# Reordering six steps of the first part's mixing stage on VectorE, ScalarE and TensorE

## The chip, the cores and the metric

The kernel runs on one core of one Trainium2 chip. The metric is the device time of one execution in microseconds (us), the median over several executions. One more execution is recorded by the hardware profiler; its trace gives start and length of each instruction on the five engines: TensorE (PE; PEld is its weight load), VectorE (DVE), ScalarE (ACT), GpSimd (POOL) and SyncE (SP, which here only issues DMAs).

## The reference, cut to what matters

Two blocks follow one another over a sequence of 512 tokens of width 1024. Each has two layers. The change lies in the first block, in the part of each layer called mixing, so it runs twice.

```
h = rms_norm(x, attn_norm[l])
proj = h @ w_in[l]
mq, mk, mv, mo, mi, mf, cq, ckv, krope, cu, cv = split_cols(proj, IN_SIZES)
qk = silu(causal_depthwise_conv(concat([mq, mk]), m_conv_w[l], m_conv_b[l]))   # 4 taps
hm = mlstm_chunkwise(q, k, v, mi + gb, mf + gb)          # 4 heads of 96
hm = sigmoid(mo) * hm
ha = mla_mixer(cq, ckv, krope, ...)                      # 6 heads, causal attention, latents 256 and 128
hc = chunk_spatial_gating(gelu(cu), gelu(cv), ...)       # 4 groups of 64
y = concat([head_rms_norm(hm), head_rms_norm(ha), head_rms_norm(hc)])
x = x + y @ w_out[l]
x = x + hier_moe(rms_norm(x, ffn_norm[l]), ...)          # 32 experts, top 2
```

The change alters no arithmetic except the order in which the eight chunks of `y @ w_out` are summed in the first half of the output columns.

## The kernel before

**Tiling.** The sequence is four token tiles of 128 (t = 0 to 3, `TT`), the width is eight chunks of 128 (k, `KC`). Everything is float32. Each engine runs its own program; all five are produced by the same Python functions, which are called once with each engine's name, so the order of the calls in `mixing` and `first_out` is the order of the work on every engine. Engines meet only at semaphores.

**PSUM banks.** In mixing a ring of six banks is handed out in call order (`next_bank`, `open_bank`). TensorE, when it opens bank number q, waits until bank q-6 has been read by the engines that are listed as its readers ("act", "dve" or "both"). So a reader that is late holds TensorE back six banks further on. At the output projection the ring has eight banks.

**Mixing, in call order.** Here are the parts that the change touches, by name.

- `lat_product` and `lat_read`: the latents. `conv_tile(i)`, i = 0 to 7: TensorE makes a 96x512 tile of the convolution's input from eight chunks, ScalarE reads the bank twice (L536 to a padded buffer `pads[i % 3]`, L537 to `conv` with bias and the last tap), VectorE adds the other three taps (L544, three instructions, from SBUF alone). ScalarE may write `pads` again once `conv_done` says that VectorE has finished tile i-3.
- `lat_turn(t)`: three transposes of a latent tile (L460), read by VectorE (L465). `gate_rows`: eight small transposes (L476), two VectorE reads (L479), one more VectorE instruction (L482), after which ScalarE takes Exp and Ln (L485, L487).
- `up_tile(t)`: the attention's up projections, four banks per token tile: two for q, one for k, one for v. ScalarE squares (L574, L587) or copies (L603), VectorE multiplies by the gain (L577, L590) and sums the squares (L593, L594), GpSimd takes the inverse root (L607, L608, L610) and signals `head_root`.
- `up_scale(t)`: VectorE alone, waits for `head_root` of its tile, then L620 to L622 and the rotation (L366 to L372).
- `gate_scans`: VectorE alone, L494 to L502. `gate_columns`: TensorE waits for the end of the scans, then eight tiny transposes (L515).
- `conv_silu`: ScalarE waits for all eight convolution tiles and applies Silu to all of them in place (L554).
- `head_turn(h)`: TensorE transposes q and k of an attention head (L638), ScalarE copies q out of its bank (L282), VectorE copies k (L284). `a_scores` of that head needs both copies.
- Then a loop of 12 steps: a token tile of v, u and v of the gating, or the output gate (`tok_tile`), two units of attention (`a_scores`, `a_turn`, `a_output`), and a third of an mLSTM head (`m_decay`, `m_scores`, `m_output`).
- The end of mixing: `norm_scale` of the gating's output `gu` (VectorE L888), `m_output(3)` (TensorE L780, VectorE L786 to L794), the last two `a_output` (L699; L704, L706), `heads_sums(2)` (ScalarE square L870, VectorE sum L874, GpSimd root L877 and L879), `gate_outputs` (VectorE L1058, four), `norm_sums` of the mLSTM output (the same lines L870, L874, L877, L879 again), `heads_scale(2)` (VectorE L888), then `out_turn` for chunks 6, 7, 3, 4, 5 (TensorE L898, even chunks read by VectorE L285, odd ones by ScalarE L282).
- `first_out`: the output projection. Its first half makes the products of the chunks `early` = (6, 7, 3, 4, 5) for four token tiles (TensorE L1071), then the transposes of chunks 0, 1, 2, then their products. VectorE adds each finished bank to `x`. The last transposes also release the first expert's weights (`big_free`, SP L1529).

All four calls of `key_rotation` run on GpSimd at the start of mixing. Waits of a queue hold all that stands behind them on that engine.

Of the kernel before, what the change touches and what calls it, by code (L numbers as in the profile page):

```python
# [8 lines left out]
TT = S // P  # L9
# [9 lines left out]
QK_TILES = 2 * M_HEADS  # L19
# [55 lines left out]
def program(nc, a):  # L75
# [5 lines left out]
    with ctx:  # L81
# [386 lines left out]
        def gate_rows(name, eng, l):  # L468

            gb = p1(l, "gate_b")  # L470
            H = slice(0, M_HEADS)
            for i, dst in ((0, log_i), (1, cum_f)):
                q, f = next_bank(name, "dve")
                if name == "pe":
                    o = 416 + i * M_HEADS
                    pe_job(eng, q, (T.transpose(bank_of(q)[H, t * P:(t + 1) * P], lat[:, t, o:o + M_HEADS], ident) for t in range(TT)))  # L476
                if name == "dve":
                    eng.wait_ge(bank_full, f + 1)
                    V.tensor_scalar(dst, bank_of(q)[H, :], gb[H, i:i + 1], None, ALU.add).then_inc(bank_read_dve, 1)  # L479
            if name == "dve":  # L480
                eng.drain()
                V.scalar_tensor_tensor(out=peak, in0=cum_f, scalar=-1.0, in1=cum_f, op0=ALU.mult, op1=ALU.min).then_inc(gate_neg, 1)  # L482
            if name == "act":
                eng.wait_ge(gate_neg, l + 1)
                A.activation(peak, peak, ACT.Exp)  # L485
                eng.drain()
                A.activation(peak, peak, ACT.Ln, bias=1.0).then_inc(gate_soft, 1)  # L487
# [36 lines left out]
        def conv_tile(name, eng, l, i, w):  # L524

            q, f = next_bank(name, "act")
            bank = bank_of(q)
            cw = p1(l, "conv_w").rearrange("p (t j) -> p t j", t=QK_TILES)
            n = l * QK_TILES + i
            if name == "pe":  # L530
                pe_job(eng, q, product(bank[M, :], lambda k: w[:, k, (i % 4) * M_DIM:(i % 4 + 1) * M_DIM], lambda k: featv[:, k, :], KC))
            if name == "act":
                eng.wait_ge(bank_full, f + 1)
                if i >= 3:
                    eng.wait_ge(conv_done, n - 2)
                A.activation(pads[i % 3][M, CONV - 1:], bank[M, :], ACT.Copy)  # L536
                A.activation(conv[M, i, :], bank[M, :], ACT.Identity, bias=p1(l, "conv_b")[M, i:i + 1],  # L537
                             scale=cw[M, i, CONV - 1:CONV]).then_inc(bank_read_act, 1)
            if name == "dve":
                if i == 0:  # L540
                    eng.wait_ge(pads_zeroed, l + 1)
                eng.wait_ge(bank_read_act, reads_of[q]["act"])
                for j in range(CONV - 1):
                    m = V.scalar_tensor_tensor(out=conv[M, i, :], in0=pads[i % 3][M, j:j + S], scalar=cw[M, i, j:j + 1],  # L544
                                               in1=conv[M, i, :], op0=ALU.mult, op1=ALU.add)
                    if j < CONV - 2:
                        eng.drain()
                m.then_inc(conv_done, 1)
# [63 lines left out]
        def up_scale(name, eng, l, t):  # L612

            if name != "dve":
                return
            half = A_ROPE // 2
            qh, kh = (v[:, t, :].rearrange("p (h w) -> p h w", w=A_QK) for v in (q_lat, k_lat))
            eng.wait_ge(head_root, l * TT + t + 1)
            rq, rk = head_ss[:, t, 0:6], head_ss[:, t, 6:12]
            V.tensor_tensor(qh, qh, rq.unsqueeze(2).to_broadcast([P, A_HEADS, A_QK]), ALU.mult)  # L620
            V.tensor_tensor(kh[:, :, 0:A_NOPE], kh[:, :, 0:A_NOPE], rk.unsqueeze(2).to_broadcast([P, A_HEADS, A_NOPE]), ALU.mult)
            V.tensor_tensor(kh[:, :, A_NOPE:], key_rope[:, t, :].unsqueeze(1).to_broadcast([P, A_HEADS, A_ROPE]),  # L622
                            rk.unsqueeze(2).to_broadcast([P, A_HEADS, A_ROPE]), ALU.mult)
            eng.drain()
            c, s = (r[:, t, :].unsqueeze(1).to_broadcast([P, A_HEADS, half]) for r in (cos1, sin1))
            work = [view(heads[:, 0, :], k * A_HEADS * half, A_HEADS, half) for k in range(4)]
            rotate(eng, qh[:, :, A_NOPE:A_NOPE + half], qh[:, :, A_NOPE + half:], c, s, work, half)
            eng.drain().then_inc(heads_scaled, 1)
# [275 lines left out]
        def mixing(name, eng, l):  # L904
# [51 lines left out]
            for t in range(TT):  # L956
                lat_turn(name, eng, l, t)
            gate_rows(name, eng, l)
            conv_tile(name, eng, l, 1, w)
            if l == 0 and name == "pe":  # L960
                eng.wait_ge(par_loaded[0], 16)
            up_tile(name, eng, l, 0)
            up_tile(name, eng, l, 1)
            conv_tile(name, eng, l, 2, w)
            up_scale(name, eng, l, 0)
            up_scale(name, eng, l, 1)
            up_tile(name, eng, l, 2)
            up_tile(name, eng, l, 3)
            gate_scans(name, eng, l)
# [6 lines left out]
            for i in range(M_HEADS, QK_TILES):  # L976
                conv_tile(name, eng, l, i, w)
            slot_done(name)
            conv_silu(name, eng, l)
            head_turn(name, eng, l, 0)  # L980
            for i in range(3 * TT):
                kind, t = ("m_val", "uv", "o")[i // TT], i % TT
                if t == 0:
# [27 lines left out]
            a_turn(name, eng, l, A_UNITS - 2)  # L1011
            a_turn(name, eng, l, A_UNITS - 1)
            gate_values(name, eng, l)
            m_output(name, eng, l, M_HEADS - 1)
            a_output(name, eng, l, A_UNITS - 2)
            a_output(name, eng, l, A_UNITS - 1)
            norm_scale(name, eng, l, gu, C_GROUPS, C_DIM, c_ss, c_norm)
            a_last = heads_sums(name, eng, l, 2)
            gate_outputs(name, eng, l)
            m_norm = norm_sums(name, eng, l, o_gate, M_HEADS, M_DIM, view(tmp, M_HEADS * S, TT, M_WIDTH), m_ss, outputs_gated(l))  # L1020
            heads_scale(name, eng, l, 2, a_last)
            if name == "pe":
                eng.wait_ge(a_out_read, (l + 1) * A_HEADS)
                set_ring(eng, range(8))
# [36 lines left out]
        def first_out(name, eng, l, m_norm):  # L1061
# [17 lines left out]
            if name == "pe":  # L1079
                y_squares.extend([0] * TT)  # L1080
                banks = [open_bank(eng, until=(half_added, l * TT + t + 1)) for t in range(TT)]
                for k in early:
                    reader = "act" if k % 2 else "dve"
                    eng.wait_ge(bank_read_act if k % 2 else bank_read_dve, reads_of[at["outT", k]][reader])
                    for t in range(TT):
                        products(banks[t], t, w, (k,))
            else:
                q = take(name, "bank", TT)
# [2 lines left out]
                out_turn(name, eng, l, o_gate, c, c, m_norm)  # L1091
            if name == "pe":
                big_free.append(count[("pe", "full")])
                eng.wait_ge(bank_read_act, reads_of[at["outT", 2]]["act"])
                eng.wait_ge(bank_read_dve, reads_of[at["outT", 2]]["dve"])
            for t in range(TT):
# [2473 lines left out]
```

## Time and profile before

| | |
|---|---|
| median of 3 executions | 3090.44 us (3090.29 to 3095.34) |
| profiled execution, its time | 3090.09 us |
| its span in the trace | 3088.3 us |
| PE busy | 2881.2 us, 93% of the span |
| DVE, ACT, POOL busy | 1133.3, 669.8, 518.6 us (37%, 22%, 17%) |
| mean granted clock of TensorE | 0.977 of full |
| mixing and first output half, first layer | about 14 to 301 us of the span |
| the same, second layer | about 659 to 939 us |

The page of the profile gives busy time by engine over the whole span; a kernel whose TensorE is busy 93% of the time still has stretches in which it waits, and these are found in the order of time. The 1.8 us between the profiled execution's time and its span lie outside the trace. In the rows a line such as "L406" is the line of a helper (here the generator that all products go through), so the place is read from the operands and the start. One product of float32 shows as two records.

### The profile page before, as it was taken

Reading aid. Unit: us, or ns where it says so; the run is one execution under the profiler, and the core shown is the slowest. Engines: PE = TensorE matmul, PEld = TensorE weight load, DVE = VectorE, ACT = ScalarE, POOL = GpSimd, SP = SyncE. Lnnn points to the kernel's source line nnn. Section 1 sums busy time; section 2 is a strip of 40 time slices with the busy share of each in tenths; the row PEclk is TensorE's granted clock in tenths of the full one; section 3 lists DMA queues with packets and bytes.
Section 4 is the critical chain, followed back from the end, with each engine's and each line's share of the span. In section 5 each row is a group of like instructions: output and inputs, shape, how many; then the busy total and the mean of one; then the engine's idle time right before and its main releaser. Section 6 shows DMA issues by size and latency. Waiting matters only on the chain.

```text
span 3088.3 us, 32675 instructions
## 1 busy us (share of the span) xinstructions
PE 2881.2 (93%) x12660; PEld 1928.4 (62%) x12660; DVE 1133.3 (37%) x2314; ACT 669.8 (22%) x1520; POOL 518.6 (17%) x789
## 2 busy tenths in 40 slices
PE   8999998889999988899999999999998899999998
PEld 4465543244656433377657488888685556688887
DVE  3534311135343111234623234344346732333354
ACT  3332210023232100101631211100204622211100
POOL 3001111121011111112310012210213610011201
PEclk9999999899999999899999999999999999999999
DMA  3113599941115999722012022222221021122122
GB/s 147 48 48 147 216 405 411 413 169 48 40 50 220 369 418 412 305 82 82 1 55 82 28 82 82 97 76 87 82 82 55 1 82 55 55 90 102 69 75 89
DMA packets 121908, 421.38 MB, mean 136 GB/s; under 512 B 9232, under 2 KB 13456, under 8 KB 95504
## 3 DMA queue, kind: packets, MB, share of 16 engines
q1 hardware_dynamic: 108528, 383.62, 32.5%
q0 software_dynamic: 12640, 33.45, 2.9%
q8 instruction: 106, 1.74, 0.2%
q10 hardware_dynamic: 576, 2.10, 0.2%
q14 instruction: 58, 0.48, 0.0%
HBM read 408.64 MB, written 27.26 MB: 141 GB/s over the span
## 4 chain that ended last, share of the span: by engine, by line
PE 81%; DMA 9%; DVE 4%; ACT 2%; issue 2%; DVEq 1%; POOLq 0%; POOL 0%; SPq 0%; ACTq 0%
PE ps L2359 33%; PE ps L406 14%; PE ps L2592 6%; DMA ring_feat<-in_w 6%; PE ps L1591 4%; PE ps L1071 4%; DMA big<-in_w 3%; PE ps L1631 2%; PE ps L2466 2%; PE ps L2612 2%; PE ps L2909 2%; PE ps L1843 1%; PE ps L1854 1%; PE ps L1866 1%; PE ps L2751 1%
## 5 line engine op out<-in xcount | busy, mean ns | idle before, releaser
L406 PE MATMUL ps<-ring_feat 128*96 128x512 f32 (+3 forms) x768 | 308.4, 558 | 11.0 <-DVE tmp L465 4.4
L2359 PE MATMUL ps<-ring_feat 128*128 128x256 f32 x1216 | 276.9, 379 | 0.8 <-ACT big L282 0.8
L2359 PE MATMUL ps<-big 128*128 128x256 f32 x1200 | 268.1, 379 | 0.0
L2359 PEld LDWEIGHTS ps<-ring_feat 128*128 128x128 f32 x1216 | 231.0, 190 | 33.4 <-issue 2.1
L2359 PEld LDWEIGHTS ps<-big 128*128 128x128 f32 x1200 | 228.0, 190 | 31.0
L406 PEld LDWEIGHTS ps<-ring_feat 128*128 128x128 f32 (+1 forms) x768 | 140.4, 185 | 163.7 <-issue 122.2
L2592 PE MATMUL ps<-ring_feat 128*128 128x512 f32 x448 | 194.6, 593 | 2.9 <-ACT ring_feat L2809 2.2
L1591 PE MATMUL ps<-big,tmp 128*64 128x512 f32 x512 | 126.3, 644 | 33.7 <-DMA big<-in_w 30.8
L2592 PEld LDWEIGHTS ps<-ring_feat 128*128 128x128 f32 x448 | 84.2, 190 | 106.7 <-issue 101.9
L1591 PE MATMUL ps<-ring_feat,tmp 128*64 128x512 f32 x512 | 125.0, 638 | 27.1 <-DMA ring_feat<-in_w 25.0
L1606 DVE TENSOR_TENSOR tmp<-tmp,ps 128x256 f32<-128x256 f32 x32 | 13.5, 421 | 327.2 <-ACT tmp L1600 327.2
L2359 PE MATMUL ps<-tmp 128*128 128x256 f32 x576 | 128.2, 379 | 0.0
L2359 PE MATMUL ps<-ring_feat,tmp 128*128 128x256 f32 x544 | 126.6, 379 | 0.0
L1071 PE MATMUL ps<-ring_feat 128*128 128x512 f32 x256 | 117.1, 610 | 1.9 <-DVE ring_feat L285 1.9
L2359 PEld LDWEIGHTS ps<-tmp 128*128 128x128 f32 x576 | 109.4, 190 | 14.9
L2359 PEld LDWEIGHTS ps<-ring_feat,tmp 128*128 128x128 f32 x544 | 103.3, 190 | 14.1
L1591 PEld LDWEIGHTS ps<-big,tmp 128*64 128x64 f32 x512 | 39.0, 147 | 113.3 <-issue 88.7
L1645 POOL DMA_INDIRECT expert_out<-tmp,route_i x32 | 32.2, 1005 | 458.6 <-ACT tmp L1640 458.6
L1591 PEld LDWEIGHTS ps<-ring_feat,tmp 128*64 128x64 f32 x512 | 38.2, 145 | 106.1 <-issue 83.4
L2359 PE MATMUL ps<-ring_feat,big 128*128 128x256 f32 x400 | 95.5, 379 | 0.0
L2548 DVE TENSOR_TENSOR big<-ps,par 128x512 f32<-128x512 f32 x32 | 22.1, 692 | 187.2 <-ACT big L2544 187.2
L1600 ACT ACTIVATE tmp<-ps 128x256 f32<-128x256 f32 x32 | 12.3, 384 | 350.8 <-PE ps L1591 350.8
(478 smaller groups left out, 4623.1 us busy)
## 6 DMA issues: line engine op xcount, KB each, us to landing
big<-in_w SPq DMA_DIRECT2D x48, 2048.0 KB, 17.9
ring_feat<-in_w SPq DMA_DIRECT2D x48, 2048.0 KB, 18.5
ring_feat<-in_w_gate_up SPq DMA_DIRECT2D x22, 2048.0 KB, 8.0
ring_feat<-in_w_mix_in SPq DMA_DIRECT2D x12, 2048.0 KB, 8.1
ring_feat<-in_w_down SPq DMA_DIRECT2D x12, 1536.0 KB, 6.8
tmp<-in_w_mem_kv SPq DMA_DIRECT2D x6, 2048.0 KB, 20.6
ring_feat<-in_w_out SPq DMA_DIRECT2D x4, 2048.0 KB, 8.6
big<-expert_out SPq DMA_DIRECT2D x16, 512.0 KB, 7.8
```

The lines of the kernel that those rows point to most:

```text
L406: yield T.matmul(bank, lhs(k), rhs(k), start=k == 0, stop=k == n - 1)
L1071: m = T.matmul(bank, featv[:, k, t * P:(t + 1) * P], w[:, k, :], start=k == 6, stop=k == 2)
L1591: m = T.matmul(ps[h, u, :], e_xT[s][:, k, h], e_up[s][k // 4][i][:, k % 4, :], start=k == 0, stop=k == KC - 1)
L1631: m = T.matmul(ps[h, 6 + half, :], e_hT[:, k, h], e_down[s][i][:, k, half * BANK:(half + 1) * BANK], start=k == 0, stop=k == 1)
L1645: eng.indirect_dma_start(out=a["expert_out"], out_offset=bass.IndirectOffsetOnAxis(ap=slots_out[:, p:p + 1], axis=0), in_=e_y[s], in_offse ...
L1843: m = T.matmul(ps[:, (n % 2) * 2 + j, :], l_qT[c % 2][h, t * P:(t + 1) * P], l_kT[c % 2][h, :], start=True, stop=True)
L1854: m = T.transpose(ps[:, 4 + j, s * P:(s + 1) * P], l_prob[n % 4][:, j, s * P:(s + 1) * P], ident)
L2359: m = T.matmul(to, lhs[:, j, :], rhs[:, j, :], start=start and j == 0, stop=stop and j == chunks - 1)
L2466: yield T.matmul(bank, featv[:, k, t * P:(t + 1) * P], w[:, k, :], start=k == 0, stop=k == KC - 1)
L2592: yield T.matmul(bank, featv[:, k, t * P:(t + 1) * P], w[:, k, :], start=k == 0, stop=k == KC - 1)
L2612: m = T.matmul(bank[:, tokens], w[:, k, (f % 4) * P:(f % 4 + 1) * P], featv[:, k, tokens], start=k == 0, stop=k == KC - 1)
L2909: m = T.matmul(bank[:, tokens], w[:, kk, o:o + P], featv[:, kk, tokens], start=kk == 0, stop=kk == KC - 1)
```

## The change

It moves six things.

1. The three VectorE instructions for convolution tile 0 leave `conv_tile(0)` and go, as a new function `conv_add`, behind `gate_rows`. The other tiles keep them at the end of `conv_tile`.
2. `conv_tile(2)` goes behind `up_scale(0)` and `up_scale(1)`. Since `up_scale` is VectorE's alone, this changes VectorE's order only.
3. `head_turn(0)` goes ahead of `conv_silu`. `conv_silu` is ScalarE's alone, so this changes ScalarE's order only.
4. `norm_scale` of `gu` goes ahead of `m_output(3)` and the last two `a_output` (VectorE only).
5. `heads_scale(2)` goes ahead of `norm_sums` of the mLSTM output (VectorE only).
6. In `first_out` the products of chunk 5 go from before the transposes of chunks 0, 1 and 2 to behind them (TensorE only).

```
             if name == "act":
                 ...
                              scale=cw[M, i, CONV - 1:CONV]).then_inc(bank_read_act, 1)
+            at["conv", i] = q
+            if i:
+                conv_add(name, eng, l, i)
+
+        def conv_add(name, eng, l, i):
+
+            cw = p1(l, "conv_w").rearrange("p (t j) -> p t j", t=QK_TILES)
             if name == "dve":
                 if i == 0:
                     eng.wait_ge(pads_zeroed, l + 1)
-                eng.wait_ge(bank_read_act, reads_of[q]["act"])
+                eng.wait_ge(bank_read_act, reads_of[at["conv", i]]["act"])
...
             gate_rows(name, eng, l)
+            conv_add(name, eng, l, 0)
             conv_tile(name, eng, l, 1, w)
...
             up_tile(name, eng, l, 1)
-            conv_tile(name, eng, l, 2, w)
             up_scale(name, eng, l, 0)
             up_scale(name, eng, l, 1)
+            conv_tile(name, eng, l, 2, w)
             up_tile(name, eng, l, 2)
...
+            head_turn(name, eng, l, 0)
             conv_silu(name, eng, l)
-            head_turn(name, eng, l, 0)
...
             gate_values(name, eng, l)
+            norm_scale(name, eng, l, gu, C_GROUPS, C_DIM, c_ss, c_norm)
             m_output(name, eng, l, M_HEADS - 1)
             a_output(name, eng, l, A_UNITS - 2)
             a_output(name, eng, l, A_UNITS - 1)
-            norm_scale(name, eng, l, gu, C_GROUPS, C_DIM, c_ss, c_norm)
             a_last = heads_sums(name, eng, l, 2)
             gate_outputs(name, eng, l)
+            heads_scale(name, eng, l, 2, a_last)
             m_norm = norm_sums(name, eng, l, o_gate, M_HEADS, M_DIM, view(tmp, M_HEADS * S, TT, M_WIDTH), m_ss, outputs_gated(l))
-            heads_scale(name, eng, l, 2, a_last)
...
-                for k in early:
+                for k in early[:-1]:
...
                 big_free.append(count[("pe", "full")])
+                k = early[-1]
+                eng.wait_ge(bank_read_act if k % 2 else bank_read_dve, reads_of[at["outT", k]]["act" if k % 2 else "dve"])
+                for t in range(TT):
+                    products(banks[t], t, w, (k,))
                 eng.wait_ge(bank_read_act, reads_of[at["outT", 2]]["act"])
                 eng.wait_ge(bank_read_dve, reads_of[at["outT", 2]]["dve"])
```

## Rows read from the trace of the kernel before

**Rows 1.** The page: the chain that ended last, shares by engine.
```profile
PE 81%; DMA 9%; DVE 4%; ACT 2%; issue 2%; DVEq 1%; POOLq 0%; POOL 0%; SPq 0%; ACTq 0%
```

**Rows 2.** Timeline of PE, first layer: start, length, what, [idle before <- releaser].
```profile
50.39 1.04 PE L476 MATMUL ps<-cst,tmp 128*4 128x128 f32 x8
53.64 7.11 PE L406 MATMUL ps<-ring_feat 128*96 128x512 f32 x16 [2.21 <-DVE tmp L465]
...
73.92 5.34 PE L406 MATMUL ps<-par,tmp 128*128 128x288 f32 x20
84.31 2.90 PE L406 MATMUL ps<-par,tmp 128*128 128x384 f32 x4 [5.05 <-DVE big L577]
...
95.73 27.71 PE L406 MATMUL ps<-ring_feat 128*96 128x512 f32 x64
```

**Rows 3.** Timeline of DVE, the same stretch.
```profile
75.41 2.39 DVE L544 SCALAR_TENSOR_TENSOR tmp<-cst,par,tmp 96x512 f32<-96x512 f32 x3 [6.31 <-ACT tmp L537]
...
83.70 0.82 DVE L577 TENSOR_TENSOR big<-ps,par 128x288 f32<-128x288 f32 x2 [0.17 <-issue]
...
92.41 0.68 DVE L502 TENSOR_TENSOR rows<-rows 4x512 f32<-4x512 f32 x1
```

**Rows 4.** Timeline of POOL, the roots of up tiles 0, 1 and 3.
```profile
67.69 2.30 POOL L610 TENSOR_TENSOR nstat<-nstat,stat 128x12 f32<-128x12 f32 x1 [0.15 <-issue]
...
70.88 2.30 POOL L610 TENSOR_TENSOR nstat<-nstat,stat 128x12 f32<-128x12 f32 x1
...
89.38 0.96 POOL L607 TENSOR_SCALAR nstat<-nstat 128x6 f32<-128x6 f32 x1
...
91.40 3.03 POOL L610 TENSOR_TENSOR nstat<-nstat,stat 128x12 f32<-128x12 f32 x1
```

**Rows 5.** Timeline of PE, second layer, the same work.
```profile
688.94 8.80 PE L406 MATMUL ps<-ring_feat 128*96 128x512 f32 x16 [2.19 <-DVE tmp L465]
...
731.67 27.71 PE L406 MATMUL ps<-ring_feat 128*96 128x512 f32 x64
...
768.06 7.02 PE L406 MATMUL ps<-ring_feat 128*128 128x384 f32 x16
```

**Rows 6.** Windows, first layer: length, busy by engine, PEclk, DMA share, GB/s.
```profile
84.00:88.00 4.00, 3.69 (x6) 1.89 (x7) 4.00 (x10) 0.98 (x2) 1.58 (x3) 0.50 0.01 4
```

**Rows 7.** Timeline of ACT, first layer, right behind convolution tile 7.
```profile
124.75 1.28 ACT L554 ACT_TABLE_LOAD   x1
```

**Rows 8.** Timeline of PE, first layer, the first two scores and the tile behind.
```profile
131.39 0.89 PE L406 MATMUL ps<-tmp 96*128 96x128 f32 x4 [1.91 <-ACT tmp L282]
132.12 5.33 PE L406 MATMUL ps<-ring_feat 128*128 128x384 f32 x16
```

**Rows 9.** Timeline of DVE, end of mixing, first layer.
```profile
257.76 1.42 DVE L888 TENSOR_TENSOR big<-big,nstat 128x256 f32<-128x256 f32 x4
...
259.87 1.97 DVE L1058 TENSOR_TENSOR big<-big,tmp 128x384 f32<-128x384 f32 x4
263.38 1.75 DVE L874 TENSOR_REDUCE nstat<-tmp 128x16 f32<-128x1536 f32 x1 [1.55 <-ACT tmp L870]
...
265.92 1.40 DVE L285 TENSOR_SCALAR ring_feat<-ps,par 128x512 f32<-128x512 f32 x2
```

**Rows 10.** Timeline of PE, the same stretch and the first output half.
```profile
259.32 1.27 PE L898 MATMUL ps<-cst,big 128*128 128x128 f32 x8 [2.20 <-DVE big L888]
...
266.96 18.99 PE L1071 MATMUL ps<-ring_feat 128*128 128x512 f32 x40
285.78 1.47 PE L898 MATMUL ps<-cst,big 128*128 128x128 f32 x12
288.19 19.12 PE L1071 MATMUL ps<-ring_feat 128*128 128x512 f32 x44 [0.94 <-DVE ring_feat L285]
```

**Rows 11.** Timeline of POOL, the root of `heads_sums(2)`.
```profile
260.68 1.74 POOL L879 TENSOR_TENSOR nstat<-nstat,stat 128x8 f32<-128x8 f32 x1
```

**Rows 12.** Timeline of ACT, the square of `heads_sums(2)`.
```profile
257.88 0.63 ACT L870 ACTIVATE big<-tmp 128x512 f32<-128x512 f32 x1 [1.30 <-DVE tmp L706]
```

More of the change, by code:

```diff
@@ L538, in conv_tile, with conv_add @@
                              scale=cw[M, i, CONV - 1:CONV]).then_inc(bank_read_act, 1)
+            at["conv", i] = q
+            if i:
+                conv_add(name, eng, l, i)
+        def conv_add(name, eng, l, i):
+            cw = p1(l, "conv_w").rearrange("p (t j) -> p t j", t=QK_TILES)
             if name == "dve":
@@ L541, in conv_tile @@
                     eng.wait_ge(pads_zeroed, l + 1)
-                eng.wait_ge(bank_read_act, reads_of[q]["act"])
+                eng.wait_ge(bank_read_act, reads_of[at["conv", i]]["act"])
                 for j in range(CONV - 1):
@@ L958, in mixing @@
             gate_rows(name, eng, l)
+            conv_add(name, eng, l, 0)
             conv_tile(name, eng, l, 1, w)
@@ L963, in mixing @@
             up_tile(name, eng, l, 1)
-            conv_tile(name, eng, l, 2, w)
             up_scale(name, eng, l, 0)
             up_scale(name, eng, l, 1)
+            conv_tile(name, eng, l, 2, w)
             up_tile(name, eng, l, 2)
@@ L978, in mixing @@
             slot_done(name)
+            head_turn(name, eng, l, 0)
             conv_silu(name, eng, l)
-            head_turn(name, eng, l, 0)
             for i in range(3 * TT):
@@ L1013, in mixing @@
             gate_values(name, eng, l)
+            norm_scale(name, eng, l, gu, C_GROUPS, C_DIM, c_ss, c_norm)
             m_output(name, eng, l, M_HEADS - 1)
@@ L1016, in mixing @@
             a_output(name, eng, l, A_UNITS - 1)
-            norm_scale(name, eng, l, gu, C_GROUPS, C_DIM, c_ss, c_norm)
             a_last = heads_sums(name, eng, l, 2)
             gate_outputs(name, eng, l)
+            heads_scale(name, eng, l, 2, a_last)
             m_norm = norm_sums(name, eng, l, o_gate, M_HEADS, M_DIM, view(tmp, M_HEADS * S, TT, M_WIDTH), m_ss, outputs_gated(l))
-            heads_scale(name, eng, l, 2, a_last)
             if name == "pe":
@@ L1081, in first_out @@
                 banks = [open_bank(eng, until=(half_added, l * TT + t + 1)) for t in range(TT)]
-                for k in early:
+                for k in early[:-1]:
                     reader = "act" if k % 2 else "dve"
@@ L1093, in first_out @@
                 big_free.append(count[("pe", "full")])
+                k = early[-1]
+                eng.wait_ge(bank_read_act if k % 2 else bank_read_dve, reads_of[at["outT", k]]["act" if k % 2 else "dve"])
+                for t in range(TT):
+                    products(banks[t], t, w, (k,))
                 eng.wait_ge(bank_read_act, reads_of[at["outT", 2]]["act"])
```

## The prediction

> **What bounds the kernel now.** I read the page first. The chain that ended last is TensorE for 81% of the span and DMA for 9% [rows 1]. So mixing, which needs no large transfer, should be paced by TensorE, and a change of order can only win what TensorE idles there. I then went through the chain in order of time over both mixing stages, and where it left TensorE I laid the engines' timelines side by side. The reader is to see four places in the first layer where TensorE waits for another engine: before convolution tile 1, 2.21 us, until VectorE has read a latent transpose; in up tile 3, 5.05 us, until VectorE has read the first bank of up tile 2 [rows 2]; before the first scores, 1.91 us, for ScalarE's copy of q [rows 8]; and around the output's transposes, 2.20 us before the first, more before the products at 266.96, and 0.94 us before the tail's products [rows 10]. The second layer has the same places. Windows show what follows a wait: from 84 to 88 us the granted clock was 0.50, the 1.2 GHz level, after TensorE had idled five microseconds [rows 6].
>
> **Edit 1, taps of tile 0 behind the gate rows.** TensorE's transposes end at 50.39 + 1.04 = 51.43. Tile 1 needs the bank of latent tile 0, the sixth before it; VectorE now reads it first, as soon as its transposes end, which is before 50.4. Tile 1 starts near 51.3 instead of 53.64: 2.35 us won [rows 2]. The taps (2.4 us by the row of tile 2 [rows 3]) now lie between the gate rows and ScalarE's reads of tile 1, where VectorE has nothing else. Cost nothing; without that cover, 2.4 us. All that hangs on tile 1 moves by 2.35, so up tile 2's first product is at 73.92 - 2.35 = 71.6.
>
> **Edit 2, two `up_scale` ahead of the taps of tile 2.** VectorE idled 6.31 us before those taps at 75.41; the taps and two `up_scale` then filled it up to 83.70, when the read came for which TensorE stood [rows 3]. The taps are 2.3, so one `up_scale` is (83.70 - 75.41 - 2.3) / 2 = 3.0. After the change `up_scale(0)` starts at root 0, which ended at 69.99 and moves to 67.65; call it 67.8. Root 1 ended 3.19 later, at 73.18 [rows 4], so 71.0 if nothing disturbs it. But it now runs beside `up_scale(0)`. The nearest rows are the roots beside the scans: the third root there took from 89.38 to 94.43, 5.05 instead of 3.19 [rows 4]. So root 1 ends between 71.0 and 72.8; the rotation's instructions are shorter than the scans, but L620 is as long as theirs, so I take 1.5 late: 72.5. Then `up_scale(1)` to 75.5, taps of tile 2 to 77.9 (ScalarE has read tile 2 by 73), up tile 2 and 3 and the scans another 93.09 - 83.70 = 9.4 [rows 3], so the gates are ready at 87.35.
>
> TensorE meanwhile: a convolution tile is 27.71 / 4 = 6.9 [rows 2]. From 71.6, six banks of up tiles (two of them of tile 3) run without a wait to 76.7; the next needs the first bank of tile 2, read by 78.4: a wait of 1.7. Two banks of 0.65 each, then tile 3 from 79.75 to 86.6, and 0.75 for the gates. `gate_columns` costs 0.6, so tile 4 starts at 87.95 instead of 95.73: **7.8 us** in layer one, of which 2.35 are edit 1's. In layer two tile 1 took 8.80 instead of 7.11, and from tile 1 to tile 4 it was 731.67 - 688.94 = 42.73 against 42.09 [rows 2, 5]; after the change both are 36.65, so layer two wins 2.35 + 6.08 = **8.4 us**. Ends of the range: root undisturbed, 1.5 more in each layer; fully disturbed and the low clock following the new 1.7 us wait, 2 less each.
>
> The Trainium skill, "SBUF — State Buffer", section "Who interferes with whom", says that a VectorE instruction with two SBUF inputs and a GpSimd instruction that reads SBUF exclude each other for the whole instruction, whoever is second waiting. The rows agree in one direction, GpSimd 3.03 instead of 2.30; in the other they do not: L502, with two SBUF inputs, ran 0.68 while L610 was under way from 91.40 [rows 3, 4]. By the rule `up_scale(0)` would be held as well.
>
> **Edit 3, q's copy ahead of Silu.** ScalarE is free at 124.75 [rows 7]. Now it waits there for the last tap; it will copy q at once (0.6) and load its table after that, still before the taps of tile 7 end. TensorE finishes its value tile before 131.39 - 1.91 = 129.48, so the scores start 1.9 to 2.1 us earlier; I take **2.0** in each layer [rows 8]. What is late next is Exp, behind Silu and a table load, at about 132.1; its first reader comes after the next value tile of 5.33, at 135.2, so nothing waits. In layer two that tile took 7.02 instead of 5.33 behind the wait [rows 5, 8], **1.7** more. Silu's own user, the mLSTM scores, comes two steps of the loop later.
>
> The attention loop is TensorE back to back in the timeline; it moves as a block.
>
> **Edits 4 and 5.** `gu` is scaled in VectorE's idle time before `m_output(3)`, so the first transposes start with TensorE's last wait for attention, near 258.0 instead of 259.32; that alone ends nothing, because the products follow chunk 6's copy by VectorE at 265.92 [rows 9, 10]. Along VectorE: the square ends at 258.51 [rows 12], the sum of the heads starts then, not behind L888, and L1058 runs from 259.35 instead of 259.87 [rows 9]. GpSimd's root, which ended at 262.42 [rows 11], ends 0.5 earlier at 261.9; `heads_scale` takes 262.0 to 262.9, in the gap of 1.55 in which VectorE waits for the square of the mLSTM output. Its sum starts at 262.95 instead of 263.38 and takes 1.75 less overlap, and the copy of chunk 6 starts at 264.6, not 265.92. The first product can start at 265.4 instead of 266.96: **1.6 us** per layer. TensorE still idles about six microseconds in pieces here, so I leave the low clock's loss as it is: 40 records took 18.99, and at the rate of the 44 behind (19.12) they take 17.4, so 1.6 are lost [rows 10]. Bounds: all of it won, or as much again lost.
>
> **Edit 6.** From the tail's transposes to its products it was 288.19 - 285.78 = 2.41, of which transposing is 1.3; the products of chunk 5 (3.4 us) now cover the copies. **1.1 us** per layer [rows 10]. No product is added. The first expert's loads are issued 3.4 us sooner in that order, with nothing else on the queues.
>
> **Sum.** Layer one 7.8 + 2.0 + 1.6 + 1.1 = 12.5; layer two 8.4 + 2.0 + 1.7 + 1.6 + 1.1 = 14.8. Together 27.3 off the profiled execution's 3090.09, which stands 0.35 under the median: **3062.8 us**, 0.9% faster. This holds if what comes behind mixing moves with it, since every load of the expert stage is issued behind a product.
>
> **The rivals.** (a) *Root 1 is not disturbed*: 1.5 more per layer, 3059.8. For it: short instructions; against it: the 5.05 of the root beside the scans [rows 4]. Chance 0.15. (b) *VectorE is held by GpSimd too*: `up_scale(0)` grows by up to one root of 2.30 per layer, 3062.8 + 4.6 = 3067.4. Against it L502 [rows 3]. 0.08. (c) *The low clock comes back elsewhere*: behind the new wait of 1.7 us, and longer at the output because the phase shifts; each time 1.6 to 1.9 us, in both layers at one or both places, 3066 to 3070. For it: a wait of 2.19 us cost layer two 1.7 and layer one nothing [rows 2, 5]. The Trainium skill, "TensorE: Matmul & The Clock Gate", section "HAM oscillation — how this bites in real kernels", likewise has idle gaps between bursts lower the clock. 0.15. (d) *The expert stage takes it back*: DMA holds 9% of the chain [rows 1], all behind mixing; if that stream were not moved, the gain would be gone, 3090. Against it: the chain reaches that stage on TensorE. 0.07. (e) *Slower*: after the gate's short wait TensorE runs the four tiles of 27.71 us at the lower level; all of them in both layers cost 55 us, 3118. It decides from 13.7 us lost per layer on; against it, the longest loss seen behind a wait is under 3 us [rows 2, 6]. 0.02.
>
> **Numbers.** Forecast 0.53, the rivals 0.47. The range 3056 to 3069 holds the forecast, (a), (b) and most of (c). Within 0.2% of before (6 us) is what a measurement can't tell from no change; (d) falls there. Faster 0.93, same 0.05, slower 0.02.
>
> **What would show it.** In the timeline of PE after: tile 1 with no idle time before it; a wait of 0.3 (a) to 2 us before the last k bank of up tile 3, for L577; under 1 us before L515; none before the first scores; L1071 starting some 1.5 us sooner after the last L780, and no wait between L898 and the tail. On POOL the second L610 near 3.0. The prediction is wrong if up tile 3 still waits 4 us or more, if the clock windows show 0.50 in new places, or if the expert stage is longer by what mixing lost.

## The result, and the profile after

The changed kernel takes 3064.08 us, median of four executions (3062.08 to 3065.95), against 3090.62 us for the kernel before (3090.29 to 3095.34, four executions). The medians are 26.5 us apart. The ratio is 0.9916 with a 95% interval of 0.9903 to 0.9930: faster by 0.84%. The forecast was 3062.8 us in a range of 3056 to 3069. The profiled execution took 3065.95 us, with a span of 3064.2.

The timeline of PE of the changed kernel, first layer, from the latents' transposes to convolution tile 4, beside [rows 2]:
```profile
49.81 1.47 PE L460 MATMUL ps<-cst,tmp 128*128 128x128 f32 x12
...
52.00 7.03 PE L406 MATMUL ps<-ring_feat 128*96 128x512 f32 x16
...
78.65 1.53 PE L406 MATMUL ps<-par,tmp 128*128 128x384 f32 x4 [1.12 <-DVE big L584]
80.02 7.03 PE L406 MATMUL ps<-ring_feat 128*96 128x512 f32 x16
87.54 0.62 PE L515 MATMUL ps<-cst,rows 4*128 4x4 f32 x8 [0.49 <-issue]
88.09 27.71 PE L406 MATMUL ps<-ring_feat 128*96 128x512 f32 x64
```
Of the two waits of 2.21 and 5.05 us one is gone and one is 1.12 us; a third, before the gates' columns, is new, 0.49 us. The group behind the long wait (two banks, k and v of up tile 3) takes 1.53 us where it took 2.90: the clock is not lowered there any more.

GpSimd's second root in the same stretch (timeline of POOL), beside [rows 4]:
```profile
68.61 0.81 POOL L614 TENSOR_SCALAR nstat<-nstat 128x6 f32<-128x6 f32 x1
69.50 0.67 POOL L615 TENSOR_SCALAR nstat<-nstat 128x6 f32<-128x6 f32 x1
70.31 2.40 POOL L617 TENSOR_TENSOR nstat<-nstat,stat 128x12 f32<-128x12 f32 x1
```
It ends 4.10 us after its first instruction began, against 3.10 in the kernel before (70.08 to 73.18). The long instruction hardly grew, 2.40 for 2.30; the two small ones in front of it did, 0.81 and 0.67 for 0.25 and 0.33. And in the timeline of DVE, `up_scale(1)` stands waiting for it:
```profile
68.55 0.76 DVE L627 TENSOR_TENSOR big<-big,nstat 128x576 f32<-128x576 f32 x1 [0.93 <-POOL nstat L617]
...
72.75 0.76 DVE L627 TENSOR_TENSOR big<-big,nstat 128x576 f32<-128x576 f32 x1 [1.35 <-POOL nstat L617]
...
75.74 2.39 DVE L551 SCALAR_TENSOR_TENSOR tmp<-cst,par,tmp 96x512 f32<-96x512 f32 x3 [0.17 <-issue]
```
The chain in order of time runs the same way: root (70.31), `up_scale(1)` (72.75), the taps of tile 2, the read of the bank (78.14), and TensorE at 78.65.

At the first head ScalarE copies q (L282) in front of Silu's table load, and TensorE's scores follow the value tile with no idle time (timelines of ACT and PE, beside [rows 7, 8]):
```profile
116.99 0.59 ACT L282 ACTIVATE tmp<-ps 96x512 f32<-96x512 f32 x1
117.60 1.28 ACT L561 ACT_TABLE_LOAD   x1
119.55 3.62 ACT L561 ACTIVATE tmp<-tmp 96x4096 f32<-96x4096 f32 x1 [0.67 <-DVE tmp L551]
```
```profile
121.67 0.82 PE L406 MATMUL ps<-tmp 96*128 96x128 f32 x4
```
At the output (timeline of PE, beside [rows 10]):
```profile
248.10 1.10 PE L905 MATMUL ps<-cst,big 128*128 128x128 f32 x8 [0.77 <-DVE tmp L713]
...
253.06 0.66 PE L905 MATMUL ps<-cst,tmp 128*128 128x128 f32 x4 [2.99 <-DVE tmp L895]
255.60 15.46 PE L1079 MATMUL ps<-ring_feat 128*128 128x512 f32 x32 [1.88 <-DVE ring_feat L285]
...
272.21 11.32 PE L1079 MATMUL ps<-ring_feat 128*128 128x512 f32 x26
```
The wait before the tail's products is gone, and the idle time ahead of the first product is three pieces instead of two.

**Stage by stage.** Both kernels' traces are cut at the same five events of TensorE and one of VectorE. The five are the first latent transpose, convolution tile 4, the first scores, `m_output(3)`, the first output product. The sixth is the first addition of an output half on VectorE. Differences of starts, in us:

```
                     layer one                      layer two
               before   after   saved  forecast   before   after   saved  forecast
to tile 4       46.65   38.28    8.37      7.8     47.27   38.30    8.97      8.4
to the scores   35.66   33.58    2.08      2.0     35.66   33.58    2.08      2.0
to m_output(3) 121.76  121.68    0.08      0      123.45  121.69    1.76      1.7
to the product  13.81   12.25    1.56      1.6     13.81   12.25    1.56      1.6
to the addition 24.08   22.82    1.26      1.1     24.41   24.29    0.12      1.1
sum            241.96  228.61   13.35     12.5    244.60  230.11   14.49     14.8
```
Mixing saved 27.8 us by the trace, with 27.3 forecast. The span shrank by 24.1: the start took 0.73 longer, from the first layer's output half to the second layer's latent transposes it took 396.46 instead of 393.36, the second layer's expert part took 1.05 less, the second block 0.96 more. All of these run unchanged instructions.

How well a stage repeats is seen where an experiment changed nothing in it. The stage to the scores took 33.58 us in all 22 layers that have edit 3, and the stage to the product 12.24 to 12.28 in all 14 that have edits 4 and 5 without added transposes. The attention loop (to `m_output(3)`) took 121.68 to 121.76 wherever the granted clock did not fall in it.

### The profile page after: what moved, and what is told of

Same layout as the page of the kernel before. It is cut to its first block, busy times and chain, and to the rows that moved or that the text cites. A ratio compares the mean times of both kernels' runs of the same rounds, so it can differ in the third digit from the quotient of the medians.

```text
span 3064.2 us, 32675 instructions
## 1 busy us (share of the span) xinstructions
PE 2873.0 (94%) x12660; PEld 1924.3 (63%) x12660; DVE 1135.9 (37%) x2314; ACT 669.6 (22%) x1520; POOL 518.6 (17%) x789
## 4 chain that ended last, share of the span: by engine, by line
PE 77%; DMA 10%; issue 5%; DVE 3%; ACT 2%; POOL 1%; POOLq 1%; DVEq 0%; SPq 0%; ACTq 0%
PE ps L2371 33%; PE ps L406 10%; DMA ring_feat<-in_w 7%; PE ps L2604 6%; PE ps L1603 4%; PE ps L1079 4%; PE ps L1643 2%; PE ps L2478 2%; PE ps L2624 2%; PE ps L2921 2%; DMA big<-in_w 2%; PE ps L1866 1%; PE ps L1855 1%; PE ps L1878 1%; PE ps L2763 1%
```

## The experiments

Each kernel is the changed kernel with one edit, and each is read by the stages above (layer one, layer two). Where one time is given it is that of one execution. The kernel before took 3089.38 us beside the first four, 3087.47 beside the next four, and 3090.65 (median of seven) beside the last four.

**Edit 1 taken out.**
```
             gate_rows(name, eng, l)
-            conv_add(name, eng, l, 0)
...
-            if i:
-                conv_add(name, eng, l, i)
+            conv_add(name, eng, l, i)
```


> The changed kernel with edit 1 alone taken out: VectorE's taps of convolution tile 0 stand ahead of the latents' reads again. If edit 1 paid on its own and nothing later absorbs it, TensorE waits about 2.2 us for L465 before convolution tile 1 in each layer and all behind it moves by that much: from the first latent transpose to convolution tile 4 it is 38.3 + 2.2 = 40.5 us in layer one, and 40.5 to 42.2 in layer two (the low clock behind the wait cost 1.7 there before). Time 3064 + 4.4 to 6.1, so 3068 to 3071. Rival, that VectorE's chain from up tile 1 to the scans sets the end and has room: then part of the 2.2 is absorbed in the waits of 1.12 and 0.49 us that are left, the stretch is 38.3 to 39.5, and the time 3064 to 3067.

Measured: 3072.25 us; to tile 4 42.18 and 40.44. The timeline of PE, first layer, has the old wait, and this time the low clock behind it in layer one (8.80, where [rows 2] had 7.11), while layer two has none:
```profile
52.56 8.80 PE L406 MATMUL ps<-ring_feat 128*96 128x512 f32 x16 [2.20 <-DVE tmp L465]
...
80.74 1.53 PE L406 MATMUL ps<-par,tmp 128*128 128x384 f32 x4 [0.86 <-DVE big L583]
```
The wait of 2.2 comes back in full and the later one shrinks from 1.12 to 0.86 only. So hardly anything is absorbed, and the rival falls. In the kernel before it was layer two whose tile 1 took 8.80, behind the same wait; now it is layer one. So the wait costs 2.1 us for certain, and in two layers of four 1.7 more. (Another 3.4 us of layer one were lost far behind it, in the attention loop; the last section comes back to that.)

**Edit 2 taken out.**
```
-            up_scale(name, eng, l, 0)
-            up_scale(name, eng, l, 1)
             conv_tile(name, eng, l, 2, w)
+            up_scale(name, eng, l, 0)
+            up_scale(name, eng, l, 1)
```


> The changed kernel with edit 2 alone taken out: the taps of convolution tile 2 ahead of the two up_scale again. If edit 2 brought what the sum says (7.8 - 2.35 and 8.4 - 2.35 us), the wait before the k bank of up tile 3 is back at 5.05 us in place of 1.12, the low clock behind it too, and the second GpSimd root is back at 2.30 with its two small instructions at 0.25 and 0.33: latent transposes to tile 4 takes 44.3 in layer one and 43.3 in layer two instead of 38.3 and 38.3, time 3064 + 11, so 3075. Rival, only the wait comes back and the clock stays: 42 and 42, time 3071.

Measured: 3076.01 us; to tile 4 44.28 and 44.04. The wait is 5.06 again, the group behind it 2.90 again, and the second root back at 2.30 (timelines of PE and of POOL):
```profile
82.60 2.90 PE L406 MATMUL ps<-par,tmp 128*128 128x384 f32 x4 [5.06 <-DVE big L584]
```
```profile
69.56 2.30 POOL L617 TENSOR_TENSOR nstat<-nstat,stat 128x12 f32<-128x12 f32 x1
```
Edit 2 is worth 6.0 and 5.7 us a layer, of which 3.45 are waits (5.06 against 1.12 + 0.49) and the rest, 2.3 to 2.6, the low clock behind the long wait. It is the largest of the six.

**Edit 3 taken out.**
```
-            head_turn(name, eng, l, 0)
             conv_silu(name, eng, l)
+            head_turn(name, eng, l, 0)
```


> The changed kernel with edit 3 alone taken out: ScalarE's copy of q stands behind Silu again. If edit 3 brought 2.08 us a layer, from convolution tile 4 to the first scores takes 35.66 instead of 33.58 us in both layers; if the low clock behind that wait belongs to the wait, the value tile behind it takes 7.0 instead of 5.33 us in one or both layers. Time 3064 + 4.2 to 7.5, so 3068 to 3072. Rival, the wait now overlaps another and costs nothing: 33.6 and 3064.

Measured: 3071.34 us; to the scores 35.66 in both layers, and to `m_output(3)` 123.45 and 123.44 instead of 121.69. The wait of 1.92 us is back in both layers, but the clock fell behind it in the first alone, where the value tile took 7.02. In layer two that tile took 5.33 (timeline of PE), and the 1.76 us went where TensorE had been busy without a break (window, columns as in [rows 6]):
```profile
752.21 0.89 PE L406 MATMUL ps<-tmp 96*128 96x128 f32 x4 [1.92 <-ACT tmp L282]
752.94 5.33 PE L406 MATMUL ps<-ring_feat 128*128 128x384 f32 x16
```
```profile
859.00:867.00 8.00, 8.00 (x30) 5.66 (x29) 4.04 (x13) 3.77 (x9) 0.18 (x1) 0.79 0.00 0
```
The edit is worth 2.08 a layer for certain. The kernel before and this one have four layers with this wait, and the clock fell behind it in two of them, 1.7 each.

**Edits 4, 5 and 6 taken out together** (their lines of the change reversed).

> The changed kernel with edits 4, 5 and 6 taken out together. If they brought 1.56 us up to the first product and about 1.1 behind it, from m_output(3) on TensorE to the first product takes 13.81 instead of 12.25 us, and 0.94 us of waiting are back before the tail's products, in both layers; the time is 3064 + 5.3 = 3069, give or take what the low clock does in this place (it cost 1.6 us in layer one and 3.0 in layer two of the changed kernel, 1.6 and 1.9 before). Rival, the gain at the output was given back by the low clock: then the time stays within 2 us of 3064 although the two waits are back.

Measured: 3070.95 us; to the product 13.81 and 13.81, to the addition 24.59 and 24.40. The first numbers are those of the kernel before to the hundredth. Against the changed kernel that is 3.33 us more in layer one and 1.67 in layer two. In sum the rival falls; in layer two the clock had indeed given back nearly all of edit 6 (24.40 to the addition here, 24.29 with it).

**Edit 4, then edit 5, taken out alone.**

> The changed kernel with edit 4 alone taken out: gu is scaled behind the last a_output again. VectorE's L888 then stands ahead of the heads' sum, which starts some 0.5 us later, and with it GpSimd's root; m_output(3) to the first product takes 12.25 + 0.5 = 12.75 us in both layers, time 3064 + 1. Rival, TensorE's own transposes (1.3 us later) are on the path: then it is 13.6 us.

> The changed kernel with edit 5 alone taken out: heads_scale stands behind the sum of the mLSTM output again. The sum starts as before, since it waits for ScalarE's square, and the scale (0.9 us) goes between it and the copy of chunk 6: m_output(3) to the first product takes 12.25 + 0.9 to 1.1 = 13.2 to 13.4 us, time 3064 + 2. Rival, GpSimd's root was what held heads_scale and the order is free: 12.3 us.

Measured: without edit 4 12.80 and 12.79 us to the product (3068.74 us); without edit 5 13.26 and 13.26 (3064.62 us). So edit 4 is worth 0.54 and edit 5 1.01 a layer, 1.55 in sum where both together brought 1.56. The timeline of DVE without edit 5 shows the order that costs it: sum, scale, copy.
```profile
252.30 1.75 DVE L881 TENSOR_REDUCE nstat<-tmp 128x16 f32<-128x1536 f32 x1 [1.55 <-ACT tmp L877]
253.97 0.94 DVE L895 TENSOR_TENSOR tmp<-tmp,nstat 128x128 f32<-128x128 f32 x4
254.83 1.39 DVE L285 TENSOR_SCALAR ring_feat<-ps,par 128x512 f32<-128x512 f32 x2
```
The times of these two runs differ by 4.1 us the other way round from the stages. Only 1.1 of it lies in mixing, where the kernel without edit 4 lost 1.7 in the attention loop of layer one by the low clock. At this size a single execution's time says nothing, and the stage does.

**Edit 6 taken out alone.**

> The changed kernel with edit 6 alone taken out: chunk 5's products ahead of the transposes of chunks 0, 1 and 2. The wait of 0.94 us before the tail's products is back and nothing else: m_output(3) to first product stays 12.25, first product to the first addition of the output half takes 1.1 more than at the same clock, time 3064 + 2. Rival, the order of the products also moves the low clock: a change of 1.5 us or more in that stretch.

Measured: nothing of use. This execution took 4803.23 us at a mean granted clock of 0.582, and the same kernel was run again:

> The kernel of e2_chunk5_back once more, because that execution ran at a granted clock of 0.58 throughout and says nothing. Edit 6 alone taken out: the wait of 0.94 us before the tail's products is back and nothing else: m_output(3) to first product stays 12.25, first product to the first addition of the output half is 1.1 longer at the same clock (it took 22.8 to 24.3 in the runs with edit 6, of which the low clock is 1.5 to 3.0), time 3064 + 2.

Measured: 3065.30 us; to the product 12.24 and 12.24, to the addition 24.88 and 25.13. The wait is there in both layers:
```profile
274.08 1.47 PE L905 MATMUL ps<-cst,big 128*128 128x128 f32 x12
276.49 13.97 PE L1079 MATMUL ps<-ring_feat 128*128 128x512 f32 x32 [0.94 <-DVE ring_feat L285]
```
From these transposes to the tail's products it is 2.41 us against 1.31 with edit 6, so the edit is worth 1.10. The low clock, which took 15.46 - 13.90 = 1.6 us of 32 records in layer one of the changed kernel and 3.0 in layer two, took 19.78 - 17.38 = 2.4 and 2.7 of 40 here. Between layers it varies by as much as the edit brings. That is why the stage to the addition is longer here by 2.06 us in layer one and 0.84 in layer two.

**The second root without company.** Is it VectorE that makes that root slower?
```
-            eng.wait_ge(head_root, l * TT + t + 1)
+            eng.wait_ge(head_root, l * TT + (2 if t == 0 else t + 1))
```


> The changed kernel, but up_scale(0) waits for the roots of both token tiles, so that VectorE does nothing while GpSimd takes the second root. If VectorE's instructions with two SBUF inputs are what made that root's three instructions 0.81, 0.67 and 2.40 us, they are 0.25, 0.33 and 2.30 here, from 68.61 to 71.8 instead of 72.71. VectorE then does both up_scale in 6 us from there, to 77.9 instead of 75.6, and the wait before the k bank of up tile 3 grows from 1.12 to about 3.3 us; conv 38.3 + 2.2 = 40.5 us, time 3064 + 4 to 8, by what the clock does. Rival, GpSimd is slower by itself in this place (just behind another root): then the root still ends at 72.7, the wait is 4.2 and the stretch 41.4.

Measured: 3070.32 us; to tile 4 42.74 and 41.63. The root (timeline of POOL):
```profile
67.81 0.24 POOL L614 TENSOR_SCALAR nstat<-nstat 128x6 f32<-128x6 f32 x1
68.13 0.33 POOL L615 TENSOR_SCALAR nstat<-nstat 128x6 f32<-128x6 f32 x1
68.61 2.30 POOL L617 TENSOR_TENSOR nstat<-nstat,stat 128x12 f32<-128x12 f32 x1
```
It takes 3.10 us from its start instead of 4.10. So the slowing belongs to what VectorE does meanwhile; the rival, GpSimd slow by itself, falls. TensorE's wait grew to 3.19 and 3.30 us as expected, and the low clock came with it in both layers, which the stage (42.7 and 41.6 against 40.5 expected) shows.

**`up_scale(1)` behind the scans.** If the last two waits hang on `up_scale(1)` waiting for the root, then it should not stand there.
```
             up_scale(name, eng, l, 0)
-            up_scale(name, eng, l, 1)
             conv_tile(name, eng, l, 2, w)
...
             gate_scans(name, eng, l)
+            up_scale(name, eng, l, 1)
             conv_tile(name, eng, l, 3, w)
```


> The changed kernel with up_scale(1) moved again, from before the taps of tile 2 to behind the scans. VectorE then does up_scale(0) to 71.4, waits for ScalarE's reads of tile 2 (73.7), has the taps done at 76.1 and the first bank of up tile 2 read at 76.5, before TensorE asks for it at 77.5; the scans end at 85.5, before tile 3's products at 85.8. So both waits that are left, 1.12 and 0.49 us, go, and the disturbed second root no longer matters: conv 38.28 - 1.75 = 36.5 us in both layers, time 3064 - 3.5 = 3060.5. Rival: the 3 us that VectorE now does behind the scans make the taps of tiles 3 and 4 late, and something behind (ScalarE's pads, the first head) waits: conv 36.5, but head more than 33.58, and the time 3062 to 3066.

Measured: 3061.11 us (3059.23 to 3062.08), ratio to the kernel before 0.9902, interval 0.9885 to 0.9918. To tile 4 36.40 and 36.39, to the scores 33.58 in both. All of TensorE's instructions there now follow without idle time:
```profile
71.91 6.63 PE L406 MATMUL ps<-par,tmp 128*128 128x288 f32 x24
78.38 7.03 PE L406 MATMUL ps<-ring_feat 128*96 128x512 f32 x16
85.34 0.65 PE L515 MATMUL ps<-cst,rows 4*128 4x4 f32 x8
85.92 6.25 PE L406 MATMUL ps<-ring_feat 128*96 128x512 f32 x14
```
The stage is shorter by 1.9 us in each layer, by the expected mechanism and nearly the expected size (1.75). The expected rival, a wait further on, did not come. In time the gain over the changed kernel is 3 us by medians, but the two intervals overlap (0.9885 to 0.9918 and 0.9903 to 0.9930). The changed kernel was not run beside it, so by time alone it is not shown.

**TensorE kept busy at the output.**
```
+                for _ in range(24 if chunk == 5 else 0):
+                    T.transpose(bank_of(q)[:, 0:P], ident, ident)
                 eng.wait_ge(out_scaled, k + 1)
...
+                for _ in range(16):
+                    T.transpose(banks[0][:, 0:P], ident, ident)
                 for k in early[:-1]:
```


> The changed kernel with idle stretches of TensorE at the output filled: 24 transposes of the identity into the opened bank of chunk 5 ahead of its wait, and 16 into the first output bank ahead of the first product; both banks are overwritten by the work that follows, so the output is the same. At full clock they take 2.7 and 1.8 us of the 2.99 and 1.88 us idle. If the low clock is the answer to the idle time, it is not granted any more and the half from the first product to the first addition takes 21.3 us in both layers instead of 22.8 and 24.3, with m_output(3) to first product unchanged at 12.25: time 3064 - 4.5 = 3059.5. Rival: the low clock comes anyway (the idle 0.77 us and the transposes before are enough), the added transposes run at half speed and overrun their gaps: m_output(3) to first product 13 to 15 us, half unchanged, time 3066 to 3069.

Measured: 3063.01 us (3058.60 to 3063.27), ratio 0.9905, interval 0.9889 to 0.9922. To the product 15.52 and 14.02 us, to the addition 21.26 and 21.26. Neither expectation had it right, and the timeline of PE (first layer) shows why:
```profile
250.02 2.78 PE L905 MATMUL ps<-cst 128*128 128x128 f32 x24
253.17 0.66 PE L907 MATMUL ps<-cst,tmp 128*128 128x128 f32 x4 [0.37 <-DVE tmp L895]
255.71 3.43 PE L1093 MATMUL ps<-cst 128*128 128x128 f32 x16 [1.88 <-DVE ring_feat L285]
258.98 13.90 PE L1081 MATMUL ps<-ring_feat 128*128 128x512 f32 x32
```
The 24 filled their gap. The 16 did not: opening four output banks in a ring of eight, with five taken by the transposes, makes the fourth wait for chunk 6's bank to be read, and that is the same VectorE copy for which the first product waits. So they ran behind the wait and delayed the products, 3.43 us where the low clock met them, 1.94 in layer two where it did not come. The sum of both stages, 36.8 and 35.3 us, is no better than 35.1 and 36.5 of the changed kernel. The experiment is inconclusive on whether full filling would keep the clock up: with one of the gaps filled it stayed up in one layer of two.

**Both together.**

> Both of e3_scale1_late and e3_filled: if they are independent, 3064 - 3.5 - 4.5 = 3056 us and a ratio to the kernel before of 0.989. Rival, that each pays only in the trace and the rest of the program takes it back: the ratio stays within the interval of the changed kernel, 0.990 to 0.993.

Measured: 3060.29 us (3057.23 to 3064.23), ratio 0.9905, interval 0.9888 to 0.9921. To tile 4 36.39 and 36.40; to the product 15.29 and 15.64; to the addition 21.67 and 21.30. The added 16 took 3.25 and 3.60 us, so here the low clock met them in both layers; over the two filled kernels it stayed away in one layer of four. The rearranged `up_scale` keeps its 1.9 us a layer and the added transposes bring nothing. Neither expectation is decided by the time, since the interval overlaps that of each single edit. `up_scale(1)` behind the scans, without filling, is the version to keep by the traces.

## Why the prediction was right, step by step

**What bounds it.** Right. At equal clock every stage grew again by what its edit had won when that edit was taken out, and only 0.26 us (edit 1) was absorbed elsewhere.

**Edit 1.** Right: 51.3 forecast for tile 1; it starts 2.19 us after the latents' first transpose, where it stood 4.56 behind it before, so 2.37 won, 2.35 forecast. "Cost nothing" has a crack. The gate rows' last VectorE instruction (L482) now meets GpSimd's 128x512 product (timelines of DVE and POOL, first layer):
```profile
54.20 1.63 DVE L482 SCALAR_TENSOR_TENSOR rows<-rows 4x512 f32<-4x512 f32 x1 [0.50 <-issue]
55.76 2.39 DVE L551 SCALAR_TENSOR_TENSOR tmp<-cst,par,tmp 96x512 f32<-96x512 f32 x3
```
```profile
54.00 1.28 POOL L956 TENSOR_TENSOR par<-par,cst 128x512 f32<-128x512 f32 x1
```
It took 0.68 before and takes 1.63, and 1.88 in layer two. With edit 1 taken out the two do not meet, and it takes 0.68 again (same timelines):
```profile
55.32 0.68 DVE L482 SCALAR_TENSOR_TENSOR rows<-rows 4x512 f32<-4x512 f32 x1
```
```profile
53.09 1.28 POOL L955 TENSOR_TENSOR par<-par,cst 128x512 f32<-128x512 f32 x1
```
In all 22 layers in which they meet, L482 ends 0.54 to 0.56 us behind the end of that product, whether it began 0.2 us behind the product's start, as in layer one, or a few hundredths ahead of it, as in layer two. ScalarE's Ln ends 0.6 us before its first read of tile 1, so it cost nothing by that margin.

**Edit 2.** The mechanism was right and the size of one term a little off: the second root was taken 1.5 late and was 1.0 late (it ended 4.19 behind the first instead of 3.19), inside the bounds 0 and 1.85. TensorE's wait was 1.12 instead of 1.7, so that the k bank came 0.5 earlier than forecast, and the wait before the gates' columns was 0.49 instead of 0.75. That makes the difference of 0.6 us between 7.8 and 8.37, and between 8.4 and 8.97. Where the root loses its time was forecast wrongly: by the sign on record its long instruction should have taken near 3.0 us, and it took 2.40, while the two small ones beside L627 and L628 lost 0.9. The scans were a poor neighbour to read it from. Rival (a), no disturbance, fell: the root with no company shows what it would have been. Rival (b), VectorE held by GpSimd in `up_scale(0)`, fell in this place: L627 takes 0.76 there and 0.76 in `up_scale(1)`. But by L482 the rule of the Trainium skill, "SBUF — State Buffer", section "Who interferes with whom", by which either side can be the one that waits, agrees with the trace elsewhere, and the prediction was too quick to set one direction aside on L502 alone. For the long root the trace does not bear out the rule's other half, that the second waits for the whole instruction: while L617 ran from 70.31 to 72.71, VectorE's rotation with two SBUF inputs (L367 to L372) took 0.24 to 0.26 us a piece, as long as with no root beside it. That L956 holds L482 is read from their ends; no run takes L956 away.

**Edit 3.** Right, 2.08 for 2.0, and 1.76 for the 1.7 of clock in layer two. The second term rests on the one trace of before: it counts a fall of the clock that came in two of four layers with this wait, so that it is 1.7 and not nothing or twice as much is luck of that trace. The same holds for the 1.7 behind tile 1 in edit 1.

**Edits 4 and 5.** Right: 1.56 for 1.6, split into 0.54 and 1.01.

**Edit 6.** The order is worth 1.10, as forecast. To the addition layer one won 1.26 and layer two 0.12, because the low clock took 3.0 us of layer two's products instead of the 1.6 that was left standing. Windows of the changed kernel, second layer (columns as in [rows 6]):
```profile
879.00:881.00 2.00, 0.30 (x1) 0.34 (x2) 2.00 (x3) 0.84 (x2) 0.88 (x2) 0.71 0.00 0
881.00:883.00 2.00, 2.00 (x3) 0.84 (x3) 0.21 (x1) 0.00 (x0) 2.00 (x1) 0.50 0.00 0
883.00:885.00 2.00, 2.00 (x3) 0.68 (x2) 1.66 (x4) 0.00 (x0) 1.06 (x2) 0.50 0.32 35
885.00:887.00 2.00, 2.00 (x4) 0.87 (x3) 0.31 (x1) 0.00 (x0) 0.00 (x0) 0.59 0.75 287
```
TensorE is busy 0.30 of the first 2.00 us, and through the uninterrupted products behind that the granted clock is 0.50, the lower level of 1.2 GHz. In the kernel before the clock took 1.6 us of the 40 records in layer one and 1.9 in layer two, not 1.6 in both as the sum has it. Rival (c), the low clock coming back elsewhere, is thus a part of the outcome, with 1.1 us and not 3 to 7. Behind the new wait (0.86 to 1.33 us) it did not come in any of the 16 layers that have it.

**The sum.** Mixing 27.8 for 27.3. That is closer than its terms: up to tile 4 it won 1.1 more than forecast in the two layers together, and at the addition 0.8 less, and these have different causes. The time came out 1.3 us above the forecast. Rival (e), tiles at the lower level behind the gates' wait, did not happen: the four tiles took 27.71 as before. Rival (d), the expert stage taking the gain back, did not happen; whether it took two or three microseconds is open. From the first output half's first addition to the next layer's first transpose it was 393.36 in the one trace of the kernel before, and 393.0 to 397.0 in twelve traces with the reordered mixing or part of it, eleven of them above 394.8. But all that lies outside the ten stages of the table together was 2603.5 us before and 2600.0 to 2607.3 in those twelve, 2604.8 on average. One trace of before is too little to tell a loss of 1.3 us from chance in a spread of 7. The windows of the routing part do not settle it: from before to after the clock was lower in layer one and higher in layer two, as the lengths were 3.10 us more and 1.05 less. Before:
```profile
341.00:366.00 25.00, 21.47 (x97) 17.89 (x96) 14.67 (x61) 4.81 (x9) 2.78 (x4) 0.86 0.51 173
978.00:1008.00 30.00, 25.52 (x109) 21.61 (x108) 15.81 (x64) 4.90 (x10) 3.54 (x5) 0.79 0.45 155
```
After:
```profile
328.00:353.00 25.00, 22.21 (x95) 18.60 (x95) 14.32 (x61) 3.52 (x8) 2.57 (x3) 0.82 0.44 164
954.00:984.00 30.00, 25.43 (x112) 20.54 (x113) 17.23 (x72) 4.89 (x10) 4.37 (x5) 0.83 0.50 174
```

## What to carry to other kernels

When TensorE waits for a PSUM bank, look not at the engine that reads it but at what stands ahead of that read in its queue, and whether some of it could have run in an earlier idle time of the same engine; here 6.31 us of VectorE's idle time lay four microseconds ahead of the wait of 5.05 that its queue caused.

A wait on TensorE may cost more than itself by the low clock behind it. Ahead of convolution tile 1, up tile 3 and the first scores, the clock fell behind all six waits of 3.2 to 5.1 us and cost 1.5 to 3.0; behind four of eight waits of 1.9 to 2.2 us, 1.7; and behind none of 16 of 0.86 to 1.33 us. Which of the like waits pays changes from trace to trace and from layer to layer. So an edit of 1 to 2 us should be judged by the length of its stage between two fixed events in the trace, not by one time, and a lower clock should be looked for where it fell before it is put down to a wait.

Before filling idle time with other work, check that the work does not stand behind the same wait.

## What the runs showed of the hardware that was not expected

- **The lower clock without idle time.** In the first layer of the kernel with `up_scale(1)` behind the scans, the granted clock fell in the middle of the attention loop, with TensorE busy 8.00 us of 8.00 in this window and in every one since 112 us; the stage took 123.38 instead of 121.69:
```profile
152.00:160.00 8.00, 8.00 (x32) 4.38 (x31) 2.41 (x8) 1.13 (x4) 0.00 (x0) 1.00 0.00 0
160.00:168.00 8.00, 8.00 (x22) 3.81 (x22) 1.73 (x6) 2.40 (x6) 0.00 (x0) 0.79 0.00 0
```
  The same stage was also 1.7 us longer in layer one without edit 4 and in layer two without edit 3, and 3.4 longer in layer one without edit 1. In each the fall stands in a window in which TensorE was busy 8.00 of 8.00 us. No edit of those kernels reaches into it.
- **VectorE and GpSimd slow each other by turns.** GpSimd's two small instructions went from 0.25 and 0.33 to 0.81 and 0.67 us beside `up_scale(0)`, its long one only from 2.30 to 2.40; VectorE's L482 went from 0.68 to 1.63 and 1.88 us beside GpSimd's 1.28 us product, ending 0.55 us behind it each time.
- **A whole execution at the lower clock.** One of the 14 profiled executions ran at a mean granted clock of 0.582 and took 4803 us, with the kernel before at 3087.47 in the same session. VectorE's and ScalarE's busy times in it (1144.8 and 673.3 us) are within 1% of the usual ones: only TensorE (4719.1 us busy instead of 2873.0) was much slower.
